# Two transformer stacks in one kernel: projection sums moved among the last attention heads, mixer levels taken by units, cross scores among the values

## The reference, cut to what matters

```python
for i in range(2):                      # first block
    u = rms_norm(h, g); z = u @ w_in    # q, k, v, gate of two attentions of 8 heads x 64, forget gate
    oa = forgetting_attention(norm(qa), norm(ka), va, log_sigmoid(fa)) * silu(ga)
    ob = dilated_attention(rope(norm(qb)), rope(norm(kb)), vb) * silu(gb)
    h = h + concat([oa, ob]) @ w_out
    h = h + (p_i @ w_ple) * sigmoid(rms_norm(h, g2) @ w_gate)
for l in range(2):                      # second block
    x = x + 0.5 * swiglu(rmsnorm(x))    # d_ff 2816
    q, f, i, g, ub = split(rmsnorm(x) @ w_in)
    o_a = hgrn2_mixer(q, f, i, g)       # gated recurrence, 4 heads of 128
    o_b = multiscale_pool(ub)           # trailing means over 2, 4, 8, 16 tokens, then a map
    x = x + concat([o_a, o_b]) @ w_out
    x = x + mem_cross_attention(rmsnorm(x), rmsnorm(mem))   # 4 heads of 256, 256 memory rows
    x = x + 0.5 * swiglu(rmsnorm(x))
return rmsnorm(x, final_norm)
```

## Time and profile before

| | |
|---|---|
| median of 3 runs | 3203.68 us (3202.72 to 3211.57) |
| the profiled execution | 3203.93 us, its span 3202.1 us |
| mean granted TensorE clock | 0.975 |
| busy TensorE / VectorE / ScalarE / GpSimd | 3085.8 / 1643.5 / 1105.6 / 67.2 us |

### The profile page before, as it was taken

One profiled execution on the slowest core, in us unless ns is written; L12 is line 12 of the kernel. 1 busy time (PEld: TensorE's weight loads), 2 busy tenths in 40 slices (PEclk: granted clock), 3 DMA queues, 4 the chain that ended last, 5 costly groups with the idle time before them and its releaser, 6 DMA issues.

```text
span 3202.1 us, 33710 instructions
## 1 busy us (share of the span) xinstructions
PE 3085.8 (96%) x14426; PEld 2544.1 (79%) x14426; DVE 1643.5 (51%) x1870; ACT 1105.6 (35%) x1312; POOL 67.2 (2%) x70
## 2 busy tenths in 40 slices
PE   8999999999999999889999999999999889999998
PEld 6787877878888887778788888888878778688886
DVE  4554555455654556355444545545465364454545
ACT  5434444344422226324332222322235233432222
POOL 0000000000000000110000000000000200000000
PEclk9999999999999999889999999999999799999999
DMA  4121221202233223103322232222332014223221
GB/s 148 40 70 38 87 86 57 66 27 92 92 107 107 92 102 110 51 14 106 105 92 92 93 105 92 92 92 94 104 119 93 14 40 137 74 92 103 95 92 66
DMA packets 41494, 270.56 MB, mean 84 GB/s; under 512 B 5728, under 2 KB 5984, under 8 KB 9984
## 3 DMA queue, kind: packets, MB, share of 16 engines
q1 hardware_dynamic: 41344, 268.40, 24.4%
HBM read 266.22 MB, written 2.10 MB: 84 GB/s over the span
## 4 chain that ended last, share of the span: by engine, by line
PE 80%; DVE 11%; ACT 7%; issue 1%; DVEq 1%; DMA 0%; SPq 0%; ACTq 0%
PE PS L216 23%; PE PS L218 22%; PE PS L217 22%; DVE w_lo L201 4%; ACT w_hi L193 3%; PE PS L875 2%; PE PS L1602 2%; DVE XT L1094 2%; PE PS L529 2%; PE PS L864 1%; DVE total L280 1%; PE PS L1851 1%; PE PS L1826 1%; PE PS L501 1%; DVEq L1518 1%
## 5 line engine op out<-in xcount | busy, mean ns | idle before, releaser
L193 ACT ACTIVATE w_hi<-w_raw 128x2048 fp32r<-128x2048 f32 x242 | 463.5, 1915 | 1237.1 <-PE PS L218 1232.9
L201 DVE TENSOR_TENSOR w_lo<-w_raw,w_hi 128x2048 fp32r<-128x2048 f32 x242 | 554.6, 2292 | 413.0 <-ACT w_hi L193 412.0
L216 PE MATMUL PS<-uh_b,w_hi 128*128 128x512 f32 x1312 | 511.8, 390 | 0.0
L218 PE MATMUL PS<-uh_b,w_lo 128*128 128x512 f32 x1312 | 510.6, 389 | 0.0
L217 PE MATMUL PS<-ul_b,w_hi 128*128 128x512 f32 x1312 | 510.5, 389 | 0.0
L216 PE MATMUL PS<-w_hi,uh_a 128*128 128x512 f32 x768 | 306.6, 399 | 20.3 <-DVE ul_a L271 11.1
L216 PE MATMUL PS<-uh_a,w_hi 128*128 128x512 f32 x800 | 313.6, 392 | 8.1 <-DVE ul_a L496 6.2
L217 PE MATMUL PS<-ul_a,w_hi 128*128 128x512 f32 x800 | 312.0, 390 | 0.0
L218 PE MATMUL PS<-uh_a,w_lo 128*128 128x512 f32 x800 | 311.9, 390 | 0.0
L217 PE MATMUL PS<-w_lo,uh_a 128*128 128x512 f32 x768 | 302.3, 394 | 0.0
L218 PE MATMUL PS<-w_hi,ul_a 128*128 128x512 f32 x768 | 301.4, 392 | 0.0
(11 more groups left out here) (290 smaller groups left out, 3833.7 us busy)
## 6 DMA issues: line engine op xcount, KB each, us to landing
w_raw<-in_weights SPq DMA_DIRECT2D x242, 1024.0 KB, 4.8
XT<-in_xT SPq DMA_DIRECT2D x8, 256.0 KB, 8.4
mem_raw<-in_mem SPq DMA_DIRECT2D x2, 1024.0 KB, 4.7
out<-XT SPq DMA_DIRECT2D x8, 256.0 KB, 2.0
bands<-in_bands SPq DMA_DIRECT2D x2, 768.0 KB, 6.4
mask_numbers<-in_masks SPq DMA_DIRECT2D x1, 1152.0 KB, 7.2
p_raw<-in_pT SPq DMA_DIRECT2D x2, 512.0 KB, 3.9
lb<-in_lb_logits SPq DMA_DIRECT2D x2, 512.0 KB, 5.7
```

Source lines behind the costliest of these rows:

```text
L193: act.activation(self.hi[g % 2][:], self.raw[g % 2][:], ACT.Copy).then_inc(self.hi_done.sem, 1)
L201: dve.tensor_tensor(self.lo[g % 2][:], self.raw[g % 2][:], self.hi[g % 2][:], ALU.subtract).then_inc(self.lo_done.sem, 1)
L216: pe.matmul(out, sh, mh, start=first, stop=False)
L218: return pe.matmul(out, sl, mh, start=False, stop=last)
```

## The change

- `HeadsAttention` has a `follower` (the forgetting attention: the dilated projection). In the last head TensorE makes that projection's first weight block in quarters, `first_queries(0)` before `turn(7)`, (1) before and (2), (3) behind `outputs(7)`, each 12 products, in banks 0 to 3. The `Angles` move into the dilated projection, behind its first splits.
- `HeadsAttention` has a `turning` (the dilated one). Chunks 0 to 2 of the mix, which the forgetting attention made, are transposed before `turn(7)`, chunk 3 behind the last outputs, chunks 4 to 7 in the middle of the first output block.
- In the mixer projection the low part of block g0 + 10 is made before Q instead of behind it.
- In the recurrence `weighed` and `keysweighed` count units and levels, and the score products of a unit wait for their own.
- `TurnInTwo` and `halves_block` take the mixer's first output block in two halves: the pooled chunks are transposed before the outputs of head 3 and multiplied behind them, then the recurrent chunks.
- The values of the cross attention go to banks 4 to 7; scores 0 and 1 stand behind the first two of their four blocks, maxima, exponentials and divisions of heads 0 and 1 between the weight splits. (`exps`, `maxes`, `divide` and `scores` become methods with their bodies unchanged; this isn't shown.)

```diff
+    def halves_block(self, pe):
+        w, turn = self.k.w, self.turn
+
+        def tile(c):
+            for f in range(2):
+                i = split_products(pe, self.bank(f), w.part(self.g0, c * 256 + f * P, P), [x[:, c, :] for x in self.u],
+                                   c == NT, c == NT - 1)
+            return i
+
+        w.ready(pe, self.g0)
+        pe.wait_ge(*turn.rec.kept.at(turn.rec.UNITS * HH))
+        for c in range(NT, KD):
+            pe.wait_ge(*turn.lo.at(turn.place(c)))
+            tile(c)
+        turn.recurrent(pe)
+        for c in range(NT):
+            pe.wait_ge(*turn.lo.at(turn.place(c)))
+            i = tile(c)
+        i.then_inc(w.used.sem, 1)
...
+        if self.turn:
+            self.halves_block(pe)
+        for b in range(1 if self.turn else 0, 4):
             if b >= 2:
                 pe.wait_ge(*self.feed.x.at(2 * (b - 2) + 2))
             features_block(pe, self.k.w, self.g0 + b, self.u, lambda f: self.bank(2 * b + f),
                            ready=self.u_ready if b == 0 else None, chunk_done=self.first_done if b else None)
...
+class TurnInTwo(Stage):
+    BANKS = (6, 0, 1, 2, 0, 1, 2, 3)
+    def __init__(self, sig, k, src, u, rec):
+        self.k, self.src, self.u, self.rec = k, src, u, rec
+        self.turned, self.hi, self.lo = sig("mix_turned", KD), sig("mix_hi", KD), sig("mix_lo", KD)
+    def place(self, c):
+        return (c + NT) % KD + 1
+    def hi_of(self, act, c):
+        act.wait_ge(*self.turned.at(self.place(c)))
+        act.activation(self.u[0][:, c, :], self.k.PS[:, self.BANKS[c], :], ACT.Copy).then_inc(self.hi.sem, 1)
+    def lo_of(self, dve, c):
+        dve.wait_ge(*self.hi.at(self.place(c)))
+        dve.tensor_tensor(self.u[1][:, c, :], self.k.PS[:, self.BANKS[c], :], self.u[0][:, c, :], ALU.subtract).then_inc(self.lo.sem, 1)
+    def turn(self, pe, t, c):
+        i = pe.transpose(self.k.PS[:, self.BANKS[c], t * P:(t + 1) * P], self.src[:, t, c * P:(c + 1) * P], self.k.ident)
+        if t == NT - 1:
+            i.then_inc(self.turned.sem, 1)
+    def pooled(self, pe):
+        for c in range(NT, KD):
+            for t in range(NT):
+                self.turn(pe, t, c)
+    def recurrent(self, pe):
+        pe.wait_ge(*self.lo.at(NT))
+        for t in range(NT):
+            pe.wait_ge(*self.rec.mixed.at(t + 1))
+            for c in range(NT):
+                self.turn(pe, t, c)
+    def scalar(self, act):
+        for c in range(NT):
+            self.hi_of(act, c)
+    def vector(self, dve):
+        for c in range(NT):
+            self.lo_of(dve, c)
 class Turn(Stage):
-    def __init__(self, sig, k, src, u, src_done, early=None):
-        self.k, self.src, self.u, self.src_done, self.early = k, src, u, src_done, early
+    BANKS = (0, 1, 2, 3, 0, 1, 2, 6)
+    def __init__(self, sig, k, src, u, att):
+        self.k, self.src, self.u, self.att = k, src, u, att
         self.turned, self.hi, self.lo = sig("mix_turned", KD), sig("mix_hi", KD), sig("mix_lo", KD)
-    def bank(self, c):
-        return (c + 4) % 8
+    def hi_of(self, act, c):
+        act.wait_ge(*self.turned.at(c + 1))
+        act.activation(self.u[0][:, c, :], self.k.PS[:, self.BANKS[c], :], ACT.Copy).then_inc(self.hi.sem, 1)
+    def lo_of(self, dve, c):
+        dve.wait_ge(*self.hi.at(c + 1))
+        dve.tensor_tensor(self.u[1][:, c, :], self.k.PS[:, self.BANKS[c], :], self.u[0][:, c, :], ALU.subtract).then_inc(self.lo.sem, 1)
+    def turn(self, pe, c):
+        for t in range(NT):
+            i = pe.transpose(self.k.PS[:, self.BANKS[c], t * P:(t + 1) * P], self.src[:, t, c * P:(c + 1) * P], self.k.ident)
+        i.then_inc(self.turned.sem, 1)
     def scalar(self, act):
         for c in range(KD):
-            act.wait_ge(*self.turned.at(min(c + 5, KD) if self.early else c + 1))
-            act.activation(self.u[0][:, c, :], self.k.PS[:, self.bank(c), :], ACT.Copy).then_inc(self.hi.sem, 1)
+            self.hi_of(act, c)
     def vector(self, dve):
-        for c in range(KD):
-            dve.wait_ge(*self.hi.at(c + 1))
-            dve.tensor_tensor(self.u[1][:, c, :], self.k.PS[:, self.bank(c), :], self.u[0][:, c, :], ALU.subtract).then_inc(self.lo.sem, 1)
+        for c in range(NT, KD):
+            self.lo_of(dve, c)
     def tensor(self, pe):
-        def turn(t, cs):
-            for c in cs:
-                i = pe.transpose(self.k.PS[:, self.bank(c), t * P:(t + 1) * P], self.src[:, t, c * P:(c + 1) * P], self.k.ident)
-                if t == NT - 1:
-                    i.then_inc(self.turned.sem, 1)
-        if self.early:
-            pe.wait_ge(*self.early[0].at(self.early[1]))
-            for t in range(NT):
-                turn(t, range(4, KD))
-        for t in range(NT):
-            pe.wait_ge(*self.src_done[0].at(self.src_done[1][t]))
-            turn(t, range(4 if self.early else KD))
+        pe.wait_ge(*self.att.pt_act.at(NH))
+        self.turn(pe, 3)
     def ready(self, pe, k):
-        pe.wait_ge(*self.lo.at(max(k + 1, 2)))
+        pe.wait_ge(*self.lo.at(k + 1))
+        if k == 0:
+            pe.wait_ge(*self.att.pt_dve.at(NH))
+        if k == NT - 1:
+            pe.wait_ge(*self.att.mixed.at(NH))
+            for c in range(NT, KD):
+                self.turn(pe, c)
...
         self.gains = (2, 3) if dilated else (0, 1)
+        self.angles = Angles(sig, m, opening) if dilated and layer == 0 else None
...
         w.split_hi(act, g0 + 1)
+        if self.angles:
+            self.angles.scalar(act)
         if self.rows:
...
         w.split_lo(dve, g0 + 1)
+        if self.angles:
+            self.angles.vector(dve)
         if self.rows:
...
+    def first_queries(self, pe, t):
+        for c in range(4):
+            i = split_products(pe, self.k.PS[:, t, :], [x[:, c, t * P:(t + 1) * P] for x in self.u],
+                               self.k.w.part(self.g0, c * 512, 512), c == 0, False)
+        if t == NT - 1:
+            i.then_inc(self.k.w.used.sem, 1)
     def tensor(self, pe):
...
-        project(0, 0, 0)
         if self.rows:
+            project(0, 0, 0)
             self.rows.sums(pe)
...
                 finish(h - 1)
+        if self.turning:
+            for c in range(NT):
+                self.turning.lo_of(dve, c)
         finish(NH - 1)
...
                 pe.wait_ge(*self.g_out.at(1))
+            if self.follower and h == NH - 1:
+                self.k.w.ready(pe, self.follower.g0)
+                pe.wait_ge(*self.scores.shifted.at(NH))
+                self.follower.first_queries(pe, 0)
+            if self.turning and h == NH - 1:
+                pe.wait_ge(*self.scores.shifted.at(NH))
+                for c in range(3):
+                    self.turning.turn(pe, c)
             turn(h)
...
                 outputs(h - 1)
+        if self.follower:
+            self.follower.first_queries(pe, 1)
         outputs(NH - 1)
+        if self.follower:
+            self.follower.first_queries(pe, 2)
+            self.follower.first_queries(pe, 3)
...
         dve.tensor_tensor(m.G[:], m.G[:], m.hnorm[:].unsqueeze(1).to_broadcast(full), ALU.mult).then_inc(self.hnorm.sem, 1)
+        w.split_lo(dve, g0 + 10)
         w.wait_used(dve, g0 + 9)
         dve.tensor_tensor(m.Q[:], k.PS[:, 4:8, :], k.R[:].unsqueeze(1).to_broadcast(full), ALU.mult).then_inc(self.qread.sem, 1)
-        w.split_lo(dve, g0 + 10)
...
                 e = right(m.E[h % 2][:, n, :], n, 0)
-                i = pool.tensor_tensor(e, e, right(m.Kf[h % 2][:], n, 0), ALU.mult)
-            i.then_inc(self.keysweighed.sem, 1)
+                pool.tensor_tensor(e, e, right(m.Kf[h % 2][:], n, 0), ALU.mult).then_inc(self.keysweighed.sem, 1)
...
         for h in range(HH):
+            if h == HH - 1:
+                for c in range(NT, KD):
+                    self.turn.hi_of(act, c)
             act.wait_ge(*self.out.at(h + 1))
...
                 e = right(E[:, n, :], n)
-                dve.tensor_tensor(e, e, right(m.Q[:, h, :], n), ALU.mult)
-            dve.tensor_tensor(E[:, LEVELS, :], E[:, LEVELS, :], m.Q[:, h, :], ALU.mult)
-            dve.drain()
-            dve.sem_inc(self.weighed.sem, 1)
+                i = dve.tensor_tensor(e, e, right(m.Q[:, h, :], n), ALU.mult)
+                if n % 2 or n == LEVELS - 1:
+                    i.then_inc(self.weighed.sem, 1)
+            dve.tensor_tensor(E[:, LEVELS, :], E[:, LEVELS, :], m.Q[:, h, :], ALU.mult).then_inc(self.weighed.sem, 1)
...
                 weigh(h + 1)
+            else:
+                for c in range(NT, KD):
+                    self.turn.lo_of(dve, c)
             finish(h)
...
         def scores(h):
-            pe.wait_ge(*self.weighed.at(h + 1))
-            pe.wait_ge(*self.keysweighed.at(h + 1))
             W = m.E[h % 2]
             for unit in range(self.UNITS):
+                pe.wait_ge(*self.weighed.at(self.UNITS * h + unit + 1))
+                pe.wait_ge(*self.keysweighed.at(LEVELS * h + min(2 * unit + 2, LEVELS)))
```

(54 more changed lines are left out.)

81 lines of the change are left out of this document (40 added, 41 removed).

## The result

The changed kernel takes 3131.7 us, median of 4 runs (3122.14 to 3146.46), against 3206.93 us, median of 4 runs of the kernel before on the same chip: ratio 0.9765, 95% interval 0.9739 to 0.9791. Unchanged, it was measured twice more beside the experiments, at 3127.29 us (0.9746, 0.9729 to 0.9764) and 3124.38 us (0.9739, 0.9726 to 0.9752). The forecast was 3120.0, so the median lies 4 to 12 us above it.

What follows compares the result with a forecast made beforehand. TensorE, busy 96% of the span, was taken as the bound, with time to win in idle stretches and slow-clock work behind them. Six parts summed to 86.7 us, less 3 for falls: 84, giving 3120 us, range 3109 to 3146.

Steps and rivals of the forecast that it cites:

- Part 1: Last forgetting-attention head: first queries of the dilated projection fill TensorE's idle stretch; 8.7 us a layer, 17.4 in all.
- Part 2: Last dilated head: turning the mix in pieces fills the gaps; 5.5 us in layer 0, 5.8 in layer 1.
- Part 3: Mixer projection's opening: low split before Q cuts a 3.30 us wait to 1.1; 15 us, less 1.5 a layer.
- Part 4: Recurrence head 0: score products wait by units and levels; 10.7 us a layer, 21.4 in all, 3.4 if the clock falls.
- The first rival: The clock falls all the same in the mixer, costing 11 us a layer: 3142 us; chance 0.12.
- Part 5: Mixer's first output block in two halves behind the last recurrence head; 7.0 us a layer, 14 in all.
- Part 6: Cross attention: scores 0 and 1 among the values; 3.8 us a layer, 7.6 in all.
- The rival of 3135: The clock gives back less: a third of some 46 us is paced by ScalarE and VectorE anyway; chance 0.05.
- the 3134: Time if the skill's 1% ramp penalty bound the clock's share to at most 32 us of the sum.
- late splits: Next block's low part comes late in parts 1, 2 and 5, up to 2.3 us at six places: 3134; chance 0.07.
- nothing won: Filled waits were covering VectorE work that then ends the stages as before: 3204 us; chance 0.03.
- slower: Interleaved weak products bring the low clock over whole attention loops and recurrences; 220 us more of it give 3219; chance 0.03.

Runs made afterwards that it cites:

- The filled gap: Changed kernel plus four unused 512-column products before the wait for the first kept unit in recurrence head 0, both layers: 3123.27 us, 0.9736 of the kernel before.
- parts 1 and 3 undone: Two runs of the changed kernel: without the dilated projection's early quarters, 3146.28 us (0.9812); with the mixer projection's low split behind Q again, 3134.55 us (0.9774).
- part 4 undone: Changed kernel with a head's score products waiting at unit 0 for all weighings of the head: 3144.13 us, 0.9809 of the kernel before.

## Why the prediction was right, and which term was off

The mechanism was right: each part, undone alone, gives back its wait and, in most layers, slow work behind it. The sum of 84 us stands against 77.7 us in the stages. Against the kernel before, measured beside it each time, the three medians give 75, 81 and 84 us. That the profiled span comes out at just 3120 is partly luck: 4 us of it lie outside the stages.

- **Part 1** (17.4 forecast, 16.4 measured): TensorE at clock 1.00 from 160.06 to 177.17, largest wait 0.47 us.
- **Part 2** (11.3, 12.0): 18.55 us without an idle one; all three gaps (1.12, 1.27 and 1.34 us) are filled.
- **Part 3** (12, 12.0): the wait fell to 1.1 us, and the short fall for which I had taken off 1.5 us a layer is there, 3.4 us long.
- **Part 4** (21.4, 14.1): the term that was mis-sized, by 7.3 us, and more than the whole difference between the sum of 84 and the 77.7. The order of the work came as foreseen, and the wait of 1.2 us for `kept` too. I let the clock hold over it. It fell for 10.2 us in both layers. The filled gap gives the 10.7 us a layer of the forecast (36.5 to 25.8), so the term that was off is the one with the condition "if the clock holds". The first rival was thus true of head 0; in the opening its fall was the short one that the sum already held (3.4 us); its price of 7.3 us a layer for head 0 was twice what the gap cost, 3.6.
- **Part 5** (14, 13.1): the products ran over the sums, root and scalings, 15.65 us against 15.2. The tightest point, the next block's low part, came in time.
- **Part 6** (7.6, 10.1): the wait for `Pm` is gone. The fall behind that wait went with it in both layers. In layer 1 the second fall of before went too (7 us of low clock to none), though its wait, 2.03 us for `PTm`, stayed: 1.7 of the 10.1 us came by luck.
- **The clock's share.** Over the stages the low clock went from 123 to 31 us, worth half of that, 46, if it all counts, and 43 by the low clock in which TensorE was busy (114 to 29 us); the forecast had some 46. The rival of 3135, by which a third of it gives nothing back, is near the median of 3131.7, but not for its reason. The Trainium skill, "TensorE: Matmul & The Clock Gate", Part 1: The HAM clock gate, has the ramp penalty below 1% of a typical kernel span, and says so of the first products of a kernel. It sets no bound on falls in the middle of one: here half of 160 us is 2.5%, and parts 1 and 3 undone bring 31 and 20 us of low clock back. So the 3134 that the prediction drew from that figure doesn't follow from it.
- **The median** is 4 to 12 us above the forecast since falls in the attentions come in some executions and not in others. I read before's single profile as if its falls outside the change were fixed.

The other rivals: late splits didn't happen in the changed stages (the two waits of 1.8 us for a low part, at 411 and 807 us, are those of before, at 424 and 837 us); nothing won and slower are out.

## What to carry to other kernels

Price an idle stretch of TensorE by what runs behind it: here 2.2 us of gap were worth 8, and a gap of 1.1 us another 3.6, won with four products of no use. A filler product, or real work put there, is a cheap test of whether a gap costs the clock, though it can't tell the gap from the narrow products around it. Look at what ScalarE loads ahead of an activation that others wait for: one tiny activation in an idle place took a load of 1.28 us, and a wait of 1.16, out of four chains. And compare stages between two fixed products, not whole times, when the parts are near 0.3%: executions of the changed kernel spread by 24 us; its three profiled ones lie 9 us apart, and their stages 1 to 5 agree within 0.1.

## What the hardware showed that I had not expected

- Gaps of 1.1 to 1.2 us can bring the clock down, and the same gap does so in one execution and not in another (269.9 us, above). So is it with longer ones: behind 2.03 us of waiting for `PTm` the clock fell in layer 0 and held in layer 1, in all three profiles. The falls lasted from 3.4 to 24 us (the longest at 268 us, with part 4 undone). What decides it wasn't settled.
- VectorE's seven weighings take 5.78 us in head 0, beside GpSimd's, and 2.50 for head 1, where GpSimd is done. It was so before (5.77 us), and it is what the units of part 4 get around. Timeline of VectorE in the changed kernel:

```profile
1313.13 5.78 DVE L1620 TENSOR_TENSOR E<-E,Q 128x256 f32<-128x256 f32 x7 [3.69 <-ACT E L1594]
...
1328.26 2.50 DVE L1620 TENSOR_TENSOR E<-E,Q 128x256 f32<-128x256 f32 x7
```

That GpSimd is the cause is argued, not shown; no run here takes the two apart.
